# Unit products dealt out over the rows by load, and VectorE's readers one row later, in a one-core decoder layer

## The reference, cut to what matters

```
z = x @ W_in                              # 9 sections of 1024 columns
yc = cb * causal_depthwise_conv3(cc * ch) # sections CC, CH, CB
merged = sigmoid(ga) * (o @ W_a) + sigmoid(gb) * (yc @ W_b)
x1 = LayerNorm(alpha * x + merged @ W_out)
# PEER, for each token t, each of 8 heads, each of its 16 best experts e:
h = gelu(u[e] . x1[t]);  y[t] += g * h * v[e]
```

## Time and profile before

| what | value |
|---|---|
| median of 3 runs | 1784.64 us (1783.93 to 1786.53) |
| the profiled execution's own time | 1784.97 us |
| its span | 1783.2 us |
| TensorE busy | 1578.2 us, 89% of the span |
| VectorE busy | 1314.4 us, 74% |
| ScalarE busy | 779.3 us, 44% |
| bytes moved | 655.39 MB, mean 368 GB/s |

### The profile page before, as it was taken

How to read it: one execution, slowest core, us unless ns; L and a number is a source line. 1 busy time by engine, 2 the same in 40 slices (tenths; PEclk the granted TensorE clock), 3 DMA queues, 4 the chain that set the end, 5 groups by cost and what they waited for, 6 DMA issues and landing times. The chain is left out here.

```text
span 1783.2 us, 17013 instructions
## 1 busy us (share of the span) xinstructions
PE 1578.2 (89%) x5012; PEld 877.3 (49%) x5012; DVE 1314.4 (74%) x2794; ACT 779.3 (44%) x1936; POOL 494.1 (28%) x528
## 2 busy tenths in 40 slices
PE   8999999999999998989888668888898878787778
PEld 7888888866555575444344222333333323222224
DVE  4454588589988999678878886886666687766666
ACT  6567695322232225354334434444444443444453
POOL 0000000122222222324333433433333343333331
PEclk9999999999999999999899899999999999999999
DMA  5113289799999999999999999999999999999994
GB/s 204 70 69 141 96 318 397 275 422 398 420 421 421 421 391 422 424 409 419 421 412 421 421 421 422 421 421 422 421 422 420 421 395 422 421 422 421 422 421 175
DMA packets 94934, 655.39 MB, mean 368 GB/s; under 512 B 10369, under 2 KB 14209, under 8 KB 17153
## 3 DMA queue, kind: packets, MB, share of 16 engines
q0 software_dynamic: 73728, 536.90, 72.6%
q1 hardware_dynamic: 20832, 116.96, 16.8%
q10 hardware_dynamic: 288, 0.52, 0.1%
HBM read 652.25 MB, written 2.10 MB: 367 GB/s over the span
## 5 line engine op out<-in xcount | busy, mean ns | idle before, releaser
L1992 PE MATMUL psum<-uv,diag 128*128 128x512 f32 x1436 | 713.3, 627 | 188.9 <-ACT diag L968 185.0
L1481 DVE CUSTOM_DVE_ANT_0 uv<-uv,psum 128x1024 f32<-128x1024 f32 x512 | 623.1, 1218 | 294.6 <-DMA uv<-in_pk_uv,idx 287.6
L710 POOL DMA_INDIRECT uv<-in_pk_uv,idx x512 | 491.7, 960 | 1254.3 <-PE psum L1992 572.3
L1992 PEld LDWEIGHTS psum<-uv,diag 128*128 128x128 f32 x1436 | 259.8, 195 | 611.7 <-ACT diag L968 394.4
L956 ACT ACTIVATE gelu<-dots 128x1 f32<-128x1 f32 x512 | 103.5, 202 | 747.6 <-DVE dots L1481 745.5
L1897 PE MATMUL psum<-xT,raw 128*128 128x384 f32 x640 | 208.4, 486 | 0.0
L1494 DVE SCALAR_TENSOR_TENSOR oT<-uv,coef,oT 128x1024 f32<-128x1024 f32 x148 | 189.5, 1281 | 2.5 <-ACT coef L960 2.5
L1897 PEld LDWEIGHTS psum<-xT,raw 128*128 128x128 f32 x640 | 121.0, 190 | 81.5
L960 ACT ACTIVATE coef<-gelu,weight 128x1 f32<-128x1 f32 x512 | 150.9, 295 | 16.9 <-ACT gelu L956 0.2
L968 ACT ACTIVATE diag<-ident,coef 128x128 f32<-128x128 f32 x359 | 144.2, 402 | 11.7
L1733 PE MATMUL psum<-xTh,w_hi 128*128 128x512 f32 x248 | 98.7, 398 | 0.0
(11 more groups left out here) (248 smaller groups left out, 1722.7 us busy)
## 6 DMA issues: line engine op xcount, KB each, us to landing
raw<-in_w_in SPq DMA_DIRECT2D x32, 1024.0 KB, 9.0
raw_a<-in_w_a SPq DMA_DIRECT2D x12, 1024.0 KB, 4.7
raw<-in_pk_w_q SPq DMA_DIRECT2D x10, 1024.0 KB, 9.2
raw_y<-in_w_in SPq DMA_DIRECT2D x8, 1024.0 KB, 6.8
raw<-in_w_branch_a SPq DMA_DIRECT2D x8, 1024.0 KB, 9.0
uv<-in_pk_uv,idx POOLq DMA_INDIRECT x512, 14.6
raw<-in_w_out SPq DMA_DIRECT2D x6, 1024.0 KB, 10.1
raw_w<-in_pk_w_q SPq DMA_DIRECT2D x6, 1024.0 KB, 7.4
```

What stands on the lines that cost most here:

```text
L710: pool.indirect_dma_start(row_uv(r)[:], None, pk_uv, bass.IndirectOffsetOnAxis(idx[:, i % 2, j:j + 1], 0)).then_inc(row_loaded(r)[0], 16)
L1481: V.tensor_tensor_reduce(u, u, x_cur[:], 1.0, 0.0, ALU.mult, ALU.add, dots[:, r % 32:r % 32 + 1]).then_inc(dot_done, 1)
L1992: last = T.matmul(B[i][:], diag[:, n % DR, :], row_uv(r)[:, D + i * 512:D + (i + 1) * 512], start=(r in FIRST), stop=last_of_block, skip_g ...
```

## The change

It edits three places. `UNIT_ROW` no longer spreads the 304 products evenly over 58 rows (5.24 a row) but by TensorE's load, in which the query behind every fourth row up to 12 counts as 7 unit products: 3.97 unit products a row in rows 0 to 15, 5.72 in rows 16 to 57. Rows 94, 95 and 96 join `SHARED`, so VectorE adds their v, and TensorE and ScalarE no longer do. And VectorE reads the branch and output tiles three rows behind their last product in place of two. `MERGE_ROW`, `OUT_ROW`, `NORM_ROW`, `TURN_ROW` and all loads stay as they are.

```diff
         UNIT_ROW = [[-1] * UNIT_MM] * EARLY
-        UNIT_ROW += [[(UNIT_MM * n + i) * 58 // (UNIT_MM * (len(UNITS) - EARLY)) for i in range(UNIT_MM)]
-                     for n in range(len(UNITS) - EARLY)]
+        QUERY0_MM = 7
+
+        def unit_row(m):
+
+            full = (UNIT_MM * (len(UNITS) - EARLY) + QUERY0_MM * (PKH - 4)) / 58
+            slow = full - QUERY0_MM / 4
+            rows = QUERY0_ROW[PKH - 1] + 4
+            return int(m / slow if m < slow * rows else rows + (m - slow * rows) / full)
+
+        UNIT_ROW += [[unit_row(UNIT_MM * n + i) for i in range(UNIT_MM)] for n in range(len(UNITS) - EARLY)]
...
             if b == 0:
-                if r <= OUT_ROW[-1]:
+                if r <= OUT_ROW[-1] + 3:
                     return True
...
                 for n in range(16):
-                    if r == MERGE_ROW[KT * n + KT - 1] + 2:
+                    if r == MERGE_ROW[KT * n + KT - 1] + 3:
                         merge(1, n // 4, n % 4)
                 for n in range(4 * (TB - 1)):
-                    if r == OUT_ROW[KT * n + KT - 1] + 2:
+                    if r == OUT_ROW[KT * n + KT - 1] + 3:
                         residual(1, n // (TB - 1), 1 + n % (TB - 1))
```

## The result

| | before | changed |
|---|---|---|
| median, same job | 1784.68 us (14 runs) | 1787.76 us (14 runs) |
| lowest and highest | 1783.46 to 1787.38 | 1785.57 to 1791.44 |
| the profiled execution's own time, its span | 1784.97, 1783.2 | 1787.39, 1785.7 |
| TensorE, VectorE busy | 1578.2, 1314.4 | 1578.0, 1318.7 |

The ratio is 1.0015, with a 95% interval of 1.0008 to 1.0021: the change costs 3.1 us, clear of noise and under the 0.2% that the prediction counted as a change. Forecast were 1786.8 us and a chance of 0.56 for this case. The bytes are the same 655.39 MB.

A forecast was written before the change was run, and what follows sets the result against it. The DMA engines bound the kernel, so only their lack of work counts: 1.9 us at row 84 plus 0.3 before w_gate, +2.2 on 1784.97, is 1787.2; the median, 0.3 lower, is 1786.8 us, range 1780.0 to 1790.5.

The forecast's parts named there:

- What bounds the kernel: From where the rows begin, DMA engines run near 421 GB/s; only time in which they lack work can move the end.
- The one at 630 to 660 us: A stretch in which DMA falls short by 2.7 us, forecast to stay or grow by 1.9 us.
- TensorE 3.3 us late by one wait, and 1.7 more by the clock: At row 4's query TensorE idles 4.0 us, the clock drops behind it, and TensorE stays 5.0 us late.
- One of the prediction's own signs of being wrong: The prediction is wrong if the query of row 4 comes sooner than 366.85 us.
- The tie at the last unit's reader: ScalarE's read behind row 58 waits for TensorE, making row 60 2.0 us late, or 3.7 with the slower clock.
- the rows were to run ahead by up to 2.4 us: In rows 5 to 35 VectorE's reader waits vanish, filling the hole at 410 to 430 us.
- The branch readers' extra row: Last branch tile read behind row 83, paying for 3.07 us of lateness; row 84 starts 0.2 or 1.9 us later.
- The output readers and the third sum: Row 97 starts 1.8 or 3.5 us later; a third VectorE sum adds 1.2 us, so norms come 3.0 or 4.7 late.
- TensorE's first sum: A sign to look for: it comes at 690 to 692 us in place of 687.05.
- The cover is 2.5 us: Before w_gate's load, queued gathers hide 2.5 us of 2.8 us lateness, so 0.3 us is lost.
- The third rival: DMA queue runs dry before w_gate because buffers of rows 96 on free late: all 4.7 us counts, 1789.3 us; chance 0.26.
- six products spared, off the path: With rows 94 to 96 summed on VectorE, TensorE is spared six products and ScalarE three diagonals, off the path.

The follow-up runs named there:

- rows 0 to 3 full: The changed kernel with 20 unit products in rows 0 to 3, the rest by load over rows 4 to 57, three sums kept on VectorE: 1783.35 us.
- scores first: The changed kernel with ScalarE's copy of head 4's scores moved ahead of the softmax in row 3: 1786.04 us.
- the filled gap: The changed kernel with five products of a zero weight added in row 3, so TensorE works through its idle time: 1786.86 us, again 1785.99 us.
- units by load alone: The changed kernel with readers two rows behind and rows 94 to 96 on TensorE, as before the change: 1789.09 us.
- readers and sums alone: The kernel before, units spread evenly, with readers a row later and rows 94 to 96 summed on VectorE: 1783.69 us.

## Why the prediction was right

- **What bounds the kernel.** Right: the DMA engines, and only what they lack. TensorE's and VectorE's busy time hardly moved, and the loss shows as stretches under 421 GB/s: from 350 to 900 us they lack 7.4 us before and 9.8 changed. Where the holes would lie was forecast only in part. The one at 630 to 660 us was to stay or grow by 1.9 us; it shrank by 1.2, and 4.6 us are lost at 540 to 630 us.
- **TensorE 3.3 us late by one wait, and 1.7 more by the clock.** Right: 3.80 us of idle time against the 4.0 forecast, and 1.6 us of slow query in the profiled execution; TensorE begins the branch products 4.8 us late against 5.0. The prediction overlooked that the kernel before has a second gap of 1.28 us, ahead of the output products; it is in the changed kernel too (1.29 us). One of the prediction's own signs of being wrong seems to be met, since the query starts at 365.31 us and not at 366.85; but counted from row 0 it is 14.48 us against 14.49, so the forecast that it stays in place holds. Moving five products (rows 0 to 3 full) or one copy (scores first) takes it away or lessens it, and the filled gap takes the clock's part alone.
- **The tie at the last unit's reader.** Right in the size: row 61 is 3.5 us late against row 0, where row 60 was forecast 3.7. Short in the way there: the rows were to run ahead by up to 2.4 us, and row 30 is 5.1 us early (107.2 us after row 0 against 112.3). They lose this lead, and more, at seven gates' readers and not at the last alone. For the end this made no difference, as the last reader sets where the rows stand behind it.
- **The branch readers' extra row.** Right: +1.9 us forecast at row 84, +1.8 found; without the extra row it is +4.8.
- **The output readers and the third sum.** Right: row 97 3.5 and the norms behind it 4.7 us late forecast; rows 97 and 98 are 3.4 and 4.6 us late, and w_gate is issued 3.0 us later (714.33 against 711.30 us), 4.6 counted from row 0. TensorE's first sum was to come at 690 to 692 us; it came at 694.56, since that sign left out that rows 94 to 96 are VectorE's now.
- **"The cover is 2.5 us", hence 0.3 us lost before w_gate.** The term of the sum that was mis-sized: 1.7 us are lost there. Between rows 84 and 98 the changed kernel falls back by 4.6 - 1.8 = 2.8 us, as forecast, so by the prediction's own reckoning the cover was about 1.1 us. It isn't a constant either: with rows 0 to 3 full and three sums the fall back is 2.8 us again, and 2.7 us are lost. I took the difference of a gather's landing time to the shortest of a hole, 8.0 less 5.5, but the changed kernel's gathers issued at 698.6 and 701.6 us land after 8.2 us, and the engines run short nevertheless. Here a landing time did not tell how long all the engines had work. The third rival has thus a share in the result. The sum with the measured terms would be 1.8 + 1.7 = +3.5 us, on 1784.68 a time of 1788.2.
- **Forecast against the range.** 1787.76 us lies 1.0 above 1786.8, inside 1780.0 to 1790.5. In the profiled executions the difference is 1787.39 - 1784.97 = +2.4 us, against +2.2 forecast, but that they agree so closely is luck: the changed execution begins its rows 1.5 us earlier, and counted from row 0 it is 4.0 us longer. The forecast was too low mainly by the one term above.
- **What I had not seen.** That the three sums leave TensorE idle for 4.04 us before row 97, and that row 97's sum then runs at the lower clock, 3.75 us in place of 1.98. The gathers of that stretch wait for these sums. I had put them down as six products spared, off the path; how much of the 1.7 us comes from this is open.

## What to carry to other kernels

When work is spread by an engine's load, look not at the load but at the waits that the load was hiding: five products in front of a query cost nothing as long as the query's bank was not free, and all of 3.3 us once they stood behind it. An engine that is full from there on cannot make up an idle time (with 15 products in rows 0 to 3, TensorE was 3.2, 4.8 or 5.8 us late at row 58, and never less), so one gap is a delay of the whole stage, and the rows catch it wherever an in-order reader stands between them and that engine. And a gain in one stage is kept only if the queue is still full at the next place that starves; here that was the stretch before one 4 MB load.

## What the runs showed of the hardware that was not expected

- The same gap of 3.6 to 3.8 us ahead of the same query cost 1.6 us in some executions (5.43 and 5.44 us for the query) and 2.6 us in others (6.40 and 6.41), against 3.81. Both occur with the same kernel, the change, and in the execution with the slower query rows 61 and 84 come 1 us later. Whether kernels with such gaps are less even, the runs don't say: the change's 14 runs spread over 5.9 us, but the 8 of the units by load alone, with the same gap, over 2.1, and kernels without a gap of this length over 2.1 to 6.9.
- A gap of 2.16 us ahead of the output products, in the kernel with readers and sums alone, was followed by 4 us at a clock of 0.62, and by 43.37 us for work that takes 41.68 behind gaps of 1.3 us. So in this one execution even that gap cost 1.7 us, as much as the one of 3.80. The Trainium skill's page "TensorE: Matmul & The Clock Gate" (Why this matters for your kernels) advises against idle gaps between bursts of matmuls, and names a longer gap than this one. The trace agrees with the advice, and in this execution a shorter gap was enough.
